# Hybrid decoder trunk on one core: scores and values of the local attentions joined in pairs of head pairs, in other PSUM banks, with two buffers of flipped probabilities

## The chip, the core and the metric

The kernel runs on one core of one Trainium2 chip. The metric is the device time of one execution in microseconds; the median of three runs of the kernel before is 823.28 us (823.21 to 823.98).

## What is computed

Two layers of a decoder trunk on 256 tokens of width 1024. Each layer has three sub-layers, each with an RMSNorm before and after it and a residual: a hybrid mixer, a cross-attention into 256 memory tokens, and a gated feed-forward network with a short convolution. The change is in the mixer. Its input projection feeds a stick-breaking attention (4 heads of 64), a convolution module, and a dilated local attention (8 heads of 64, three windows merged), and their outputs are joined in front of one output projection:

```python
def hybrid_mixer(h, positions, w_in, ...):
    u = h @ w_in
    ...
    a_out = stick_breaking_attention(sb[:, :, 0], sb[:, :, 1], sb[:, :, 2])
    b_out = conformer_conv(...)
    q = rope(dl[:, :, 0], positions)
    k = rope(dl[:, :, 1], positions)
    c_out = dilated_mixture(q, k, dl[:, :, 2])
    return jnp.concatenate([a_out, b_out, c_out], axis=-1) @ w_out
```

With 256 tokens the three windows of the local attention come down to one softmax: a score counts as often as there are windows that hold it (0 to 3), so the exponentials are multiplied by a table of counts before they are summed.

## The kernel before

The program is written out by hand for each engine, with semaphores; no planner sets an order. All weights come as 256 groups of 512 KB through a ring of four buffers. ScalarE rounds a group to a high part (`whi`, `split_group`, L544), VectorE subtracts that for the low part (`wlo`, L955), and TensorE multiplies in three passes (high times high, high times low, low times high). A group is 24 matmuls of 256 columns where the result is wanted by feature (`transposed_product`, L1602 to L1604), 12 of 512 columns where it is wanted by token (`product`, L1585 to L1587), and 24 of 256 columns for the stick values (L1862 to L1864). TensorE frees a buffer with `w_used`; ScalarE splits run three groups ahead (`AHEAD`).

Between the weight products TensorE does the attention, in float32. The 8 local heads are taken as 4 pairs c = 0 to 3, the two heads r = 0, 1 of a pair on the upper and the lower 64 rows (or columns) of the array. For each pair:

- `dl_scores(c)` (L1717): scores of both heads, r = 0 in one bank of `psAB` and r = 1 in the other. For c > 0 each head waits for `nb_ready`, the maxima of the pair before, because the banks are the same.
- `scores_max(c)` on VectorE (L1188): adds the mask while copying the scores to SBUF (one of two buffers, by c % 2), takes the row maxima, and publishes the negated maxima (`nb_ready`).
- `exp_pair(c)` on ScalarE (L659), then `probabilities(c)` on VectorE (L1202): times the counts, sums, reciprocals (L1212, `den_ready`), then `scale_pair(c)` on ScalarE (L668, rows L673): probabilities, `p_ready`.
- `dl_flip(c)` on TensorE (L1725, rows L1532): six transposes into the two banks of `psCD`; `p_columns(c)` on ScalarE (L676) copies them to the one buffer `pT`, for which it waits until the values of the pair before are done (`o_done`).
- `dl_values(c)` on TensorE (L1730, rows L1734 and L1735): both heads into one half of the bank `accs[1][1]` (`attended`); `mixed_hi` (L683) and `mixed_lo` (L1214) take the result off in two parts for the output projection, and the next `dl_values` waits for them (`mix_lo`).

The order on TensorE: scores 0, product, scores 1, product, flip 0, scores 2, product, values 0, flip 1, scores 3, product, values 1, flip 2, first half of the stick values' weight product, values 2, stick scores 0 (`sb_scores`, L1742), second half, flip 3, product (memory keys), values 3, product, and then the cumulative sums of the stick-breaking (`sb_between`), its second pair of scores, and its values (`sb_values(0)` into `accs[0][0]`, `sb_values(1)` into `psAB[1]`). The stick scores need `sbT`, which ScalarE copies (`transposed_in`, L652) after `p_columns(2)`. VectorE has in the same stage 31 taps of the convolution (`conv_taps`, L1235, two instructions a tap) and the low parts.

Of the kernel before, what the change touches and what calls it, by code (L numbers as in the profile page):

```python
# [20 lines left out]
ACT = mybir.ActivationFunctionType  # L21
# [3 lines left out]
P = 128  # L25
DEPTH = 2
D = 1024
SEQ = 256
TOK = SEQ // P
KC = D // P  # L30
# [115 lines left out]
def hybrid_trunk(nc, x, mem, pos, consts, gains, params, pw, stream, out):  # L146
    with ExitStack() as ctx:
# [70 lines left out]
        pT = part(2 * AW).rearrange("p (h n) -> p h n", h=2)  # L218
# [48 lines left out]
        attended = accs[1][1][:, 0:SEQ]  # L267
# [91 lines left out]
        o_done = signal("o_done", DL_HEADS // 2)  # L359
# [7 lines left out]
        sbo_done = signal("sbo_done", 2)  # L367
        mix_hi = signal("mix_hi", KC)
        mix_lo = signal("mix_lo", KC)
# [158 lines left out]
        def _(act):  # L528
# [54 lines left out]
            for l in range(DEPTH):  # L583
# [180 lines left out]
                mixed_hi(4, o_done, 1, attended)  # L764
# [4 lines left out]
                mixed_hi(5, o_done, 2, attended)  # L769
# [3 lines left out]
                mixed_hi(6, o_done, 3, attended)  # L773
# [5 lines left out]
                mixed_hi(7, o_done, 4, attended)  # L779
# [6 lines left out]
                mixed_hi(0, sbo_done, 1, accs[0][0][:, 0:SEQ])  # L786
# [3 lines left out]
                mixed_hi(1, sbo_done, 2, psAB[1][:, 0:SEQ])  # L790
# [150 lines left out]
        def _(dve):  # L941
# [113 lines left out]
            for l in range(DEPTH):  # L1055
# [132 lines left out]
                def scores_max(c):  # L1188
                    w = 4 * (c % 2)
                    for r in range(2):  # L1190
# [4 lines left out]
                        for q, (a, b) in enumerate(((0, P), (P, AW))):  # L1195
                            e = dve.tensor_tensor_reduce(sms[c % 2][r][:, a:b], psAB[r][:, a:b], negm[:, a:b], 1.0,
# [17 lines left out]
                def mixed_lo(n, chunk, src, bias=None):  # L1214
                    dve.wait_ge(mix_hi.sem, mix_hi.at(l, n))
                    cols = slice(chunk * SEQ, (chunk + 1) * SEQ)
# [127 lines left out]
                mixed_lo(3, 6, attended)  # L1344
# [6 lines left out]
                mixed_lo(4, 7, attended)  # L1351
# [12 lines left out]
                mixed_lo(5, 0, accs[0][0][:, 0:SEQ])  # L1364
# [11 lines left out]
                mixed_lo(6, 1, psAB[1][:, 0:SEQ])  # L1376
# [793 lines left out]
```

## Time and profile before

| | |
|---|---|
| median of three runs | 823.28 us |
| the profiled execution | 823.6 us |
| its span | 821.5 us |
| TensorE busy | 812.9 us, 99% |
| VectorE busy | 642.5 us, 78% |
| ScalarE busy | 519.5 us, 63% |
| granted clock of TensorE | 0.999 |
| DMA | 145.69 MB, mean 177 GB/s |

The profile is of one execution. TensorE's rows show when a matmul starts and a modelled duration that overlaps the next; so the time of a group is read from its first start to the first start of what follows. A float32 matmul has two records, so that a pair of scores (four matmuls) has eight. A wait in the middle of a row's group does not show as idle time where the modelled durations cover it. The local attention of layer 0 lies between 73 and 105 us, that of layer 1 between 473 and 506 us.

### The profile page before, as it was taken

The numbers are of one execution on the slowest core, as the hardware profiler recorded it, in microseconds if no ns is written. First come the engines' busy times: TensorE is split into PE (matmuls) and PEld (weight loads), VectorE is DVE, ScalarE is ACT, GpSimd is POOL, SyncE is SP. The second block draws the span as 40 slices with busy tenths as digits, with TensorE's granted clock in tenths as the row PEclk, the third lists the DMA queues.
The fourth block names the chain that finished last, engine by engine and source line by source line (L and its number), as shares of the span: only waits on it lengthen the run. The fifth ranks groups of instructions, "written<-read, shape, count | busy, mean of one in ns | idle before, by whom it ended". The sixth has DMA issues, their size and how long they took to land.

```text
span 821.5 us, 12037 instructions
## 1 busy us (share of the span) xinstructions
PE 812.9 (99%) x4604; PEld 700.1 (85%) x4604; DVE 642.5 (78%) x1129; ACT 519.5 (63%) x809; POOL 29.2 (4%) x54
## 2 busy tenths in 40 slices
PE   8999999999999999999999999999999999999997
PEld 5998888889888888888899889888988888888885
DVE  5899986776676999998386999848677499999753
ACT  5656876566556777765365588656666477776541
POOL 2100000010010000000010000001000000000000
PEclk9999999999999999999999999999999999999999
DMA  8756344472464565556666453446535545655661
GB/s 299 282 177 182 103 128 165 144 259 99 154 233 136 172 203 193 173 197 210 200 197 239 147 154 113 141 157 204 206 121 179 189 128 180 190 174 199 223 189 51
DMA packets 40444, 145.69 MB, mean 177 GB/s; under 512 B 4594, under 2 KB 4738, under 8 KB 40388
## 3 DMA queue, kind: packets, MB, share of 16 engines
q1 hardware_dynamic: 38448, 138.38, 51.0%
q0 software_dynamic: 1936, 6.55, 2.3%
q8 instruction: 36, 0.59, 0.3%
q14 instruction: 20, 0.16, 0.1%
q10 hardware_dynamic: 4, 0.00, 0.0%
HBM read 143.87 MB, written 1.05 MB: 176 GB/s over the span
## 4 chain that ended last, share of the span: by engine, by line
PE 96%; DMA 1%; issue 1%; DVE 1%; ACT 0%; SPq 0%; DVEq 0%; POOLq 0%; POOL 0%
PE acc L1620 8%; PE acc L1587 5%; PE acc L1585 5%; PE acc L1586 5%; PE psCD L1620 4%; PE acc L1629 4%; PE acc L1602 4%; PE acc L1674 4%; PE psAB L1620 4%; PE acc L1676 4%; PE acc L1675 4%; PE acc L1603 3%; PE acc L1604 3%; PE psAB L1587 3%; PE psAB L1585 3%; PE psAB L1586 3%
## 5 line engine op out<-in xcount | busy, mean ns | idle before, releaser
L955 DVE TENSOR_TENSOR wlo<-raw,whi 128x1024 fp32r<-128x1024 f32 x240 | 287.7, 1220 | 70.6 <-ACT whi L544 68.9
L544 ACT ACTIVATE whi<-raw 128x1024 fp32r<-128x1024 f32 x240 | 249.7, 1057 | 120.0 <-PE acc L1587 45.8
L1620 PE MATMUL acc<-xT,whi 128*128 128x512 f32 x288 | 89.2, 391 | 0.0
L1620 PEld LDWEIGHTS acc<-xT,whi 128*128 128x128 f32 x288 | 54.1, 188 | 12.0
L1473 DVE SCALAR_TENSOR_TENSOR KT<-V,par,KT 128x255 f32<-128x255 f32 (+1 forms) x144 | 59.9, 478 | 1.8 <-ACT KT L888 1.2
L1629 PE MATMUL acc<-xT,wlo 128*128 128x256 f32 x288 | 58.1, 284 | 0.0
L1602 PE MATMUL acc<-xT,whi 128*128 128x256 f32 x176 | 51.0, 290 | 0.0
L1235 DVE SCALAR_TENSOR_TENSOR arena<-arena,par 128x256 f32<-128x256 f32 x120 | 50.2, 478 | 0.8 <-ACT arena L740 0.8
L1620 PE MATMUL psCD<-xT,whi 128*128 128x512 f32 x160 | 50.2, 395 | 0.0
L1603 PE MATMUL acc<-xT,whi 128*128 128x256 f32 x176 | 49.8, 283 | 0.0
L1604 PE MATMUL acc<-xT,wlo 128*128 128x256 f32 x176 | 49.8, 283 | 0.0
L471 POOL TENSOR_TENSOR stat<-stat 128x1 f32<-128x1 f32 x30 | 18.8, 626 | 777.3 <-DVE stat L1095 403.3
L1629 PEld LDWEIGHTS acc<-xT,wlo 128*128 128x128 f32 x288 | 44.8, 191 | 0.0
L1620 PE MATMUL psAB<-xT,whi 128*128 128x512 f32 x128 | 39.9, 393 | 0.0
L888 ACT ACTIVATE KT<-V,par 128x256 f32<-128x256 f32 x72 | 37.3, 595 | 0.0
L1602 PEld LDWEIGHTS acc<-xT,whi 128*128 128x128 f32 x176 | 33.7, 191 | 2.9 <-issue 2.6
L594 ACT ACTIVATE junk<-acc 128x512 bf16<-128x512 f32 x20 | 11.8, 591 | 36.9 <-PE acc L1695 22.6
L1587 PE MATMUL psAB<-whi,gT 128*128 128x512 f32 x88 | 34.3, 390 | 0.0
L1585 PE MATMUL psAB<-whi,gT 128*128 128x512 f32 x88 | 34.3, 390 | 0.0
L1586 PE MATMUL psAB<-wlo,gT 128*128 128x512 f32 x88 | 34.3, 389 | 0.0
L1603 PEld LDWEIGHTS acc<-xT,whi 128*128 128x128 f32 x176 | 33.7, 192 | 0.1
L1604 PEld LDWEIGHTS acc<-xT,wlo 128*128 128x128 f32 x176 | 33.7, 191 | 0.0
(312 smaller groups left out, 2049.0 us busy)
## 6 DMA issues: line engine op xcount, KB each, us to landing
raw<-stream_dram SPq DMA_DIRECT2D x256, 512.0 KB, 4.0
gpost<-gain_dram POOLq DMA_DIRECT2D x6, 512.0 KB, 5.1
gpre<-gain_dram POOLq DMA_DIRECT2D x5, 512.0 KB, 5.8
memn<-mem_dram SPq DMA_DIRECT2D x2, 512.0 KB, 10.8
out_dram<-h SPq DMA_DIRECT2D x4, 256.0 KB, 2.1
cst<-const_dram SPq DMA_DIRECT2D x1, 896.0 KB, 6.5
h<-x_dram SPq DMA_DIRECT2D x2, 256.0 KB, 2.8
h<-x_dram SPq DMA_DIRECT2D x1, 512.0 KB, 8.7
```

Of the source, the lines that this page charges most:

```text
L544: act.activation(home(g)[0], raw[:, s * GW:(s + 1) * GW], ACT.Copy).then_inc(w_hi.sem, 1)
L955: dve.tensor_tensor(lo, raw[:, cols], hi.bitcast(F32), ALU.subtract).then_inc(w_lo.sem, 1)
L1235: e = dve.scalar_tensor_tensor(acc, src, w, acc, ALU.mult, ALU.add)
L1473: e = dve.scalar_tensor_tensor(y[:, c, shift:SEQ], u[:, 0:SEQ - shift], par[:, PC_FW + 3 * fc + 1 - k:PC_FW + 3 * fc + 2 - k], y[:, c, shi ...
L1585: pe.matmul(outs[t], a_hi, whi[:, cols], start=k == 0, stop=False)
L1586: pe.matmul(outs[t], a_hi, wlo[:, cols], start=False, stop=False)
L1587: e = pe.matmul(outs[t], a_lo, whi[:, cols], start=False, stop=k == k_of - 1)
L1602: pe.matmul(dst, whi[:, cols], hi[:, toks], start=k == 0 and c % 2 == 0, stop=False)
L1603: pe.matmul(dst, whi[:, cols], lo[:, toks], start=False, stop=False)
L1604: e = pe.matmul(dst, wlo[:, cols], hi[:, toks], start=False, stop=k == KC - 1 and c % 2 == 1)
L1620: e = pe.matmul(up_halves(j, c), whi[:, cols], both, start=k0 + u == 0, stop=closes and u == UNITS - 1)
L1629: e = pe.matmul(up_halves(j, c)[:, 0:SEQ], wlo[:, cols], hi, start=False, stop=False)
```

## The change

It joins the scores of pairs 0 and 1 into one group on TensorE and those of pairs 2 and 3 into another, each pair of heads with banks of its own (`dl_banks`): `psAB`, `psCD`, `psAB` and both banks of `accs[1]`. Scores 1 and 3 no longer wait for maxima; scores 2 wait for those of pair 0, flip 0 for those of pair 1 (it writes the banks that hold scores 1), and values 0 for those of pair 3. The values are joined too, pairs 0 and 1 after the fourth product and pairs 2 and 3 after the first product of the memory keys, into the two halves of `attended`, and taken off by copies of 512 columns. `pT` has two buffers. The two values of the stick-breaking are joined behind the last product of the memory values, both in `psAB[1]`. On VectorE `scores_max(1)` stands right behind `scores_max(0)`, and `scores_max(3)` ahead of `probabilities(2)`. The main parts of the diff:

```diff
         sms = [[sm0[:, 0:AW], sm0[:, AW:2 * AW]], [V[:, NT:NT + AW], V[:, D + NT:D + NT + AW]]]
-        pT = part(2 * AW).rearrange("p (h n) -> p h n", h=2)
+        pT = [part(2 * AW).rearrange("p (h n) -> p h n", h=2) for _ in range(2)]
 
...
+        attended = accs[1][1]
+        sticks = psAB[1]
+
+
+        def dl_banks(c):
+
+            return (psAB, psCD, psAB, accs[1])[c]
 
 
...
                 def p_columns(c):
                     for r in range(2):
                         act.wait_ge(p_tr.sem, p_tr.at(l, 2 * c + r + 1))
-                        if c and not r:
-                            act.wait_ge(o_done.sem, o_done.at(l, c))
-                        act.activation(pT[:, r, :], psCD[r][:, 0:AW], ACT.Copy).then_inc(pT_in.sem, 1)
-
-                def mixed_hi(chunk, ready, n, src, bias=None):
+                        if c >= 2 and not r:
+                            act.wait_ge(o_done.sem, o_done.at(l, 1))
+                        act.activation(pT[c % 2][:, r, :], psCD[r][:, 0:AW], ACT.Copy).then_inc(pT_in.sem, 1)
+
+                def mixed_hi(chunk, ready, n, src, bias=None, chunks=1):
                     act.wait_ge(ready.sem, ready.at(l, n))
-                    act.activation(oT_hi[:, chunk * SEQ:(chunk + 1) * SEQ], src,
+                    act.activation(oT_hi[:, chunk * SEQ:(chunk + chunks) * SEQ], src,
                                    ACT.Copy if bias is None else ACT.Identity,
                                    bias=0.0 if bias is None else bias).then_inc(mix_hi.sem, 1)
...
                 scale_pair(1)
                 exp_pair(2)
                 split(G_SBQK + 3 + AHEAD)
-                mixed_hi(4, o_done, 1, attended)
                 p_columns(1)
                 scale_pair(2)
                 exp_pair(3)
                 split(G_SBV + AHEAD)
-                mixed_hi(5, o_done, 2, attended)
+                mixed_hi(4, o_done, 1, attended, chunks=2)
                 p_columns(2)
                 transposed_in(sbT.rearrange("p c n -> p (c n)"), [a[:, :] for a in accs[0]], G_SBQK + PER_TILE, sbT_in)
                 scale_pair(3)
-                mixed_hi(6, o_done, 3, attended)
...
-                            e = dve.tensor_tensor_reduce(sms[c % 2][r][:, a:b], psAB[r][:, a:b], negm[:, a:b], 1.0,
+                            e = dve.tensor_tensor_reduce(sms[c % 2][r][:, a:b], dl_banks(c)[r][:, a:b], negm[:, a:b], 1.0,
...
                 split(G_DLV + 3 + AHEAD)
                 dve.wait_ge(cst_in.sem, 16)
                 scores_max(0)
+                scores_max(1)
                 split(G_SBQK + AHEAD)
                 probabilities(0)
-                scores_max(1)
                 split(G_SBQK + 1 + AHEAD)
                 probabilities(1)
                 scores_max(2)
                 split(G_SBQK + 2 + AHEAD)
                 conv_taps(15, 16)
-                mixed_lo(1, 4, attended)
+                scores_max(3)
                 probabilities(2)
-                scores_max(3)
                 split(G_SBQK + 3 + AHEAD)
                 conv_taps(16, 17)
-                mixed_lo(2, 5, attended)
+                mixed_lo(1, 4, attended, chunks=2)
                 probabilities(3)
                 conv_taps(17, 19)
                 split(G_SBV + AHEAD)
...
                     for r in range(2):
-                        if c:
-                            pe.wait_ge(nb_ready.sem, nb_ready.at(l, 2 * (c - 1) + r + 1))
+                        if c == 2:
+                            pe.wait_ge(nb_ready.sem, nb_ready.at(l, r + 1))
+                        bank = dl_banks(c)[r]
                         q, k = (a[r * HD:(r + 1) * HD, c, :] for a in (dqT, dkT))
-                        pe.matmul(psAB[r][:, 0:P], q[:, 0:P], k[:, 0:P], start=True, stop=True)
-                        pe.matmul(psAB[r][:, P:AW], q[:, P:SEQ], k, start=True, stop=True).then_inc(s_done.sem, 1)
+                        pe.matmul(bank[:, 0:P], q[:, 0:P], k[:, 0:P], start=True, stop=True)
+                        pe.matmul(bank[:, P:AW], q[:, P:SEQ], k, start=True, stop=True).then_inc(s_done.sem, 1)
 
                 def dl_flip(c):
+                    if c:
+                        pe.wait_ge(pT_in.sem, pT_in.at(l, 2 * c))
+                    else:
+                        pe.wait_ge(nb_ready.sem, nb_ready.at(l, 4))
...
-                        pe.matmul(o[:, 0:SEQ], dlv[:, v0:v0 + HD], pT[:, r, 0:SEQ], start=True, stop=False)
-                        e = pe.matmul(o[:, P:SEQ], dlv[:, NT + v0:NT + v0 + HD], pT[:, r, SEQ:AW],
-                                      start=False, stop=True)
+                def dl_values(pair):
+                    for c in (2 * pair, 2 * pair + 1):
+                        pe.wait_ge(pT_in.sem, pT_in.at(l, 2 * c + 2))
+                        at = c % 2 * SEQ
+                        for r in range(2):
+                            o, v0 = attended[r * HD:(r + 1) * HD, at:at + SEQ], (2 * c + r) * HD
+                            pe.matmul(o[:, 0:SEQ], dlv[:, v0:v0 + HD], pT[c % 2][:, r, 0:SEQ], start=True, stop=False)
...
                 dl_scores(0)
+                dl_scores(1)
                 transposed_product(G_SBQK, 1, X, acc[0])
-                dl_scores(1)
                 transposed_product(G_SBQK + 1, 1, X, acc[0], k0=2)
                 dl_flip(0)
+                pe.wait_ge(dlv_in.sem, dlv_in.at(l, TOK))
                 dl_scores(2)
-                pe.wait_ge(dlv_in.sem, dlv_in.at(l, TOK))
+                dl_scores(3)
                 transposed_product(G_SBQK + 2, 1, X, acc[0], k0=4)
+                dl_flip(1)
+                transposed_product(G_SBQK + 3, 1, X, acc[0], k0=6)
+                pe.wait_ge(nb_ready.sem, nb_ready.at(l, DL_HEADS))
                 dl_values(0)
-                dl_flip(1)
-                dl_scores(3)
-                transposed_product(G_SBQK + 3, 1, X, acc[0], k0=6)
-                pe.wait_ge(mix_lo.sem, mix_lo.at(l, 1))
-                dl_values(1)
                 dl_flip(2)
 
...
                 stick_values(0)
-                pe.wait_ge(mix_lo.sem, mix_lo.at(l, 2))
-                dl_values(2)
-                pe.wait_ge(nb_ready.sem, nb_ready.at(l, DL_HEADS))
                 pe.wait_ge(sbT_in.sem, sbT_in.at(l, 2))
                 sb_scores(0)
                 stick_values(1)
                 dl_flip(3)
                 transposed_product(G_WK1, 1, M, acc[0])
-                pe.wait_ge(mix_lo.sem, mix_lo.at(l, 3))
-                dl_values(3)
+                pe.wait_ge(mix_lo.sem, mix_lo.at(l, 1))
...
                 pe.wait_ge(sbv_in.sem, sbv_in.at(l, 1))
-                pe.wait_ge(mix_lo.sem, mix_lo.at(l, 4))
+                pe.wait_ge(mix_lo.sem, mix_lo.at(l, 2))
                 product(G_WV0, 2, M, acc[1])
-                pe.wait_ge(KT_in.sem, KT_in.at(l, 4))
-                sb_values(0, accs[0][0])
                 sb_between(1)
...
-                sb_values(1, psAB[1])
```

On TensorE, at the start of the local attention (`psAB<-arena` and `psCD<-arena` are scores, `acc<-xT,whi` a weight product), before:

```order
L1587 MATMUL acc<-whi,xT 128x512
L1722 MATMUL psAB<-arena 128x128
L1723 MATMUL psAB<-arena 128x256
L1722 MATMUL psAB<-arena 128x128
L1723 MATMUL psAB<-arena 128x256
L1602 MATMUL acc<-xT,whi 128x256
```

and with the change:

```order
L1587 MATMUL acc<-whi,xT 128x512
L1723 MATMUL psAB<-arena 128x128
L1724 MATMUL psAB<-arena 128x256
L1723 MATMUL psAB<-arena 128x128
L1724 MATMUL psAB<-arena 128x256
L1723 MATMUL psCD<-arena 128x128
L1724 MATMUL psCD<-arena 128x256
L1723 MATMUL psCD<-arena 128x128
L1724 MATMUL psCD<-arena 128x256
L1602 MATMUL acc<-xT,whi 128x256
```

The eight matmuls of scores 0 and 1 stand together, the second four in `psCD`; the product that stood between them follows.

On VectorE, the end of `scores_max(0)` and what follows up to the first reciprocal of pair 0 (rows `stat<-stat 128x2` end a head's maxima or its sums), before:

```order
L1194 MEMSET stat 128x2
L1196 ISA arena,stat<-psAB,cst 128x128
L1196 ISA stat 128x1
L1196 ISA arena,stat<-psAB,cst 128x256
L1196 ISA stat 128x1
L1199 TENSOR_SCALAR stat<-stat 128x2
L955 TENSOR_TENSOR wlo<-raw,whi 128x1024
L1209 ISA arena,stat<-arena,cst 128x128
L1209 ISA stat 128x1
L1209 ISA arena,stat<-arena,cst 128x256
L1209 ISA stat 128x1
L1212 RECIPROCAL stat<-stat 128x2
```

and with the change, the same stretch, from the second head of `scores_max(1)` on:

```order
L1197 MEMSET stat 128x2
L1199 ISA V,stat<-psCD,cst 128x128
L1199 ISA stat 128x1
L1199 ISA V,stat<-psCD,cst 128x256
L1199 ISA stat 128x1
L1202 TENSOR_SCALAR stat<-stat 128x2
L958 TENSOR_TENSOR wlo<-raw,whi 128x1024
L1212 ISA arena,stat<-arena,cst 128x128
L1212 ISA stat 128x1
L1212 ISA arena,stat<-arena,cst 128x256
L1212 ISA stat 128x1
L1215 RECIPROCAL stat<-stat 128x2
```

Both heads of `scores_max(1)` (the first stands just above these rows) now come ahead of the weight split and of the probabilities of pair 0.

## Rows read from the trace of the kernel before

**Rows 1.** The page: busy time, the clock over 40 slices, the chain that ended last.
```profile
PE 812.9 (99%) x4604; PEld 700.1 (85%) x4604; DVE 642.5 (78%) x1129; ACT 519.5 (63%) x809; POOL 29.2 (4%) x54
...
PEclk9999999999999999999999999999999999999999
...
PE 96%; DMA 1%; issue 1%; DVE 1%; ACT 0%; SPq 0%; DVEq 0%; POOLq 0%; POOL 0%
```
**Rows 2.** Timeline of TensorE, layer 0. Columns: start, duration (us), engine, line, operands, count.
```profile
73.10 0.50 PE L1722 MATMUL psAB<-arena 64*128 64x128 f32 x4
...
73.97 0.39 PE L1602 MATMUL acc<-xT,whi 128*128 128x256 f32 x1
...
77.03 0.59 PE L1722 MATMUL psAB<-arena 64*128 64x128 f32 x4
...
80.96 0.82 PE L1532 MATMUL psCD<-cst,arena 128*128 128x128 f32 x6
81.71 0.50 PE L1722 MATMUL psAB<-arena 64*128 64x128 f32 x4
...
82.57 0.39 PE L1602 MATMUL acc<-xT,whi 128*128 128x256 f32 x1
...
91.95 0.88 PE L1532 MATMUL psCD<-cst,arena 128*128 128x128 f32 x6
92.58 0.36 PE L1862 MATMUL acc<-whi,xT 128*128 128x256 f32 x1
...
96.44 0.71 PE L1742 MATMUL psAB<-arena 64*128 64x256 f32 x4
...
97.30 0.39 PE L1862 MATMUL acc<-whi,xT 128*128 128x256 f32 x1
...
103.88 0.66 PE L1734 MATMUL acc<-arena 128*64 128x256 f32 x4
...
104.69 0.39 PE L1602 MATMUL acc<-mT_hi,whi 128*128 128x256 f32 x1
```
**Rows 3.** Timeline of VectorE, layer 0, from the first scores_max on.
```profile
75.22 0.06 DVE L1194 MEMSET stat<- 128x2 f32 x1
...
76.98 1.22 DVE L955 TENSOR_TENSOR wlo<-raw,whi 128x1024 fp32r<-128x1024 f32 x1
78.12 0.29 DVE L1209 CUSTOM_DVE_ANT_0 arena<-arena,cst 128x128 f32<-128x128 f32 x1
...
78.80 0.17 DVE L1212 RECIPROCAL stat<-stat 128x2 f32<-128x2 f32 x1
...
79.54 0.17 DVE L1212 RECIPROCAL stat<-stat 128x2 f32<-128x2 f32 x1
...
87.11 0.87 DVE L1235 SCALAR_TENSOR_TENSOR arena<-arena,par 128x256 f32<-128x256 f32 x2
```
**Rows 4.** Timeline of ScalarE, layer 0, scaling of pair 0 to the stick inputs.
```profile
79.00 1.55 ACT L673 ACTIVATE arena<-arena,stat 128x128 f32<-128x128 f32 x4 [0.94 <-DVE stat L1212]
...
84.47 1.48 ACT L673 ACTIVATE V<-V,stat 128x128 f32<-128x128 f32 x4
...
93.05 1.05 ACT L544 ACTIVATE whi<-raw 128x1024 fp32r<-128x1024 f32 x1
...
94.27 0.86 ACT L681 ACTIVATE arena<-psCD 128x384 f32<-128x384 f32 x2
95.00 1.09 ACT L652 ACTIVATE arena<-acc 128x512 f32<-128x512 f32 x2
```
**Rows 5.** Timelines of TensorE and VectorE, layer 1, same place.
```profile
477.76 0.48 PE L1722 MATMUL psAB<-arena 64*128 64x128 f32 x2
...
478.67 0.49 PE L1722 MATMUL psAB<-arena 64*128 64x128 f32 x2
...
483.23 0.39 PE L1722 MATMUL psAB<-arena 64*128 64x128 f32 x2
...
480.33 0.17 DVE L1212 RECIPROCAL stat<-stat 128x2 f32<-128x2 f32 x1
```

More of the change, by code:

```diff
@@ L358, in hybrid_trunk @@
         pT_in = signal("pT_in", DL_HEADS)
-        o_done = signal("o_done", DL_HEADS // 2)
+        o_done = signal("o_done", DL_HEADS // 4)
         z_done = signal("z_done", 2)
@@ L366, in hybrid_trunk @@
         a_ready = signal("a_ready", 2)
-        sbo_done = signal("sbo_done", 2)
-        mix_hi = signal("mix_hi", KC)
-        mix_lo = signal("mix_lo", KC)
+        sbo_done = signal("sbo_done", 1)
+        mix_hi = signal("mix_hi", 5)
+        mix_lo = signal("mix_lo", 5)
         rows_in = signal("rows_in", 3 * TOK)
@@ L778, in _ @@
                 split(G_WK1 + AHEAD)
-                mixed_hi(7, o_done, 4, attended)
+                mixed_hi(6, o_done, 2, attended, chunks=2)
                 split(G_WK1 + 2 + AHEAD)
@@ L789, in _ @@
                 split(G_WV0 + 3 + AHEAD)
-                mixed_hi(1, sbo_done, 2, psAB[1][:, 0:SEQ])
+                mixed_hi(0, sbo_done, 1, sticks, chunks=2)
                 for c in range(2):
@@ L1350, in _ @@
                 split(G_WK1 + AHEAD)
-                mixed_lo(4, 7, attended)
+                mixed_lo(2, 6, attended, chunks=2)
                 split(G_WK1 + 1 + AHEAD)
@@ L1728, in dl_flip @@
                         flip(psCD[r], sms[c % 2][r], 3).then_inc(p_tr.sem, 1)
-                def dl_values(c):
-                    pe.wait_ge(pT_in.sem, pT_in.at(l, 2 * c + 2))
-                    for r in range(2):
-                        o, v0 = accs[1][1][r * HD:(r + 1) * HD, :], (2 * c + r) * HD
-                        pe.matmul(o[:, 0:SEQ], dlv[:, v0:v0 + HD], pT[:, r, 0:SEQ], start=True, stop=False)
-                        e = pe.matmul(o[:, P:SEQ], dlv[:, NT + v0:NT + v0 + HD], pT[:, r, SEQ:AW],
-                                      start=False, stop=True)
+                def dl_values(pair):
[5 more added lines that the diff above has]
+                            pe.matmul(o[:, 0:SEQ], dlv[:, v0:v0 + HD], pT[c % 2][:, r, 0:SEQ], start=True, stop=False)
+                            e = pe.matmul(o[:, P:SEQ], dlv[:, NT + v0:NT + v0 + HD], pT[c % 2][:, r, SEQ:AW],
+                                          start=False, stop=True)
                     e.then_inc(o_done.sem, 1)
@@ L1754, in sb_between, with sb_values @@
                     e.then_inc(b_done.sem, 1)
-                def sb_values(c, bank):
-                    pe.wait_ge(a_ready.sem, a_ready.at(l, c + 1))
-                    for r in range(2):
-                        o, v0 = bank[r * HD:(r + 1) * HD, :], (2 * c + r) * HD
-                        a = sb_w[c][:, r * AW:(r + 1) * AW]
-                        pe.matmul(o[:, 0:SEQ], sbv[:, v0:v0 + HD], a[:, 0:SEQ], start=True, stop=False)
-                        e = pe.matmul(o[:, P:SEQ], sbv[:, SB_W + v0:SB_W + v0 + HD], a[:, SEQ:AW],
-                                      start=False, stop=True)
+                def sb_values():
+                    pe.wait_ge(a_ready.sem, a_ready.at(l, 2))
+                    for c in range(2):
+                        for r in range(2):
+                            o, v0 = sticks[r * HD:(r + 1) * HD, c * SEQ:(c + 1) * SEQ], (2 * c + r) * HD
+                            a = sb_w[c][:, r * AW:(r + 1) * AW]
+                            pe.matmul(o[:, 0:SEQ], sbv[:, v0:v0 + HD], a[:, 0:SEQ], start=True, stop=False)
+                            e = pe.matmul(o[:, P:SEQ], sbv[:, SB_W + v0:SB_W + v0 + HD], a[:, SEQ:AW],
+                                          start=False, stop=True)
                     e.then_inc(sbo_done.sem, 1)
@@ L1898, in _ @@
                 product(G_WV0 + 2, 2, M, acc[1], k0=4)
-                sb_values(1, psAB[1])
+                sb_values()
                 pe.wait_ge(ln_n.sem, ln_n.at(l, TOK))
@@ L1905, in _ @@
                     e.then_inc(ln_tb.sem, 1)
[L1907 removed]
+                pe.wait_ge(KT_in.sem, KT_in.at(l, 4))
                 product(G_OUT, 1, O, acc[0], order=MIX_ORDER)
```

18 lines of the change are left out of this document (7 added, 11 removed).

## The prediction

> **What bounds the kernel now.** I read the page first, then the order in time of TensorE, VectorE and ScalarE in the stage of the local attention. TensorE is busy for 812.9 of 821.5 us and makes up 96% of the chain that ended last [rows 1]. So only what lengthens or shortens TensorE's own stream counts. The time lies there in small groups of float32 matmuls (scores S, flips F of the probabilities, values V; S0 is the first pair of heads) between weight products of 24 matmuls.
>
> The reader is to see three things in the rows of layer 0 [rows 2]. A product of 24 takes 3.06 us up to the next small group (73.97 to 77.03). S takes 0.86 (73.10 to 73.97, and again 81.71 to 82.57), V 0.81 (103.88 to 104.69). And no small group waits visibly. That is because VectorE and ScalarE, which make the probabilities, are just in time: the scaling of pair 0 starts at 79.00 and ends at 80.55 [rows 4], and F0 starts at 80.96 [rows 2], a margin of 0.4 us. The first half of pair 1's scores, in layer 1, is where TensorE does wait: its two heads start 0.91 apart (477.76 and 478.67 [rows 5]), where in layer 0 the first four records, those of both heads, fit into 0.59 (the row at 77.03 [rows 2]). That wait is for the maxima of pair 0, since pair 1 goes to the same banks.
>
> **Part 1: S1 behind S0, S3 behind S2, in banks of their own.** The wait in layer 1 goes: it is worth 0.9 us. A joined S needs no change to or from the weight product. Its cost in that place is on no row: at most the 0.86 of S, at least the streaming alone. A head streams two records of 128 columns and two of 256, six units of 128, both heads side by side; F has six transposes of 128 columns too and takes 0.63 up to a product (91.95 to 92.58). I take 0.75, midway, since nothing speaks for either end, and the same for a joined V. Little rests on it: most joined groups come ahead of a wait that takes the difference up, and two a layer (V3 and the joined stick values) are left on the path.
> The Trainium skill, TensorEngine Tiling (Array Packing), Key Properties, says that a change of tiling mode drains TensorE; by it a joined group would cost its streaming alone, and with 0.63 for the four groups on the path the sum below would be 828.4 instead of 828.9. No row here shows a joined pair.
> Without waits, TensorE's small groups shrink by about 0.1 for each of two S, two V and the stick values, and by 0.1 to 0.2 for each of the changes to and from a weight product that go with S1, V1 and V2: about 1.0 us a layer, an estimate, 2.0 in all, 2.9 with the wait of layer 1.
>
> **Part 2: the maxima of pair 1 move ahead of the probabilities of pair 0 on VectorE.** This decides. One scores_max takes 1.76 us (75.22 to 76.98 [rows 3]). It now stands before the weight split and the denominators of pair 0, so the reciprocal that ends at 78.97 (78.80 + 0.17) ends at 80.73. ScalarE's scaling, which already waited 0.94 for it [rows 4], starts at 80.76, and its halves (1.55 / 2, the second one released 0.74 later as the reciprocals are, 78.80 to 79.54) end at 81.54 and 82.31. TensorE reaches F0 at about 80.6, because S1 is joined. Its two flips start at 81.6 and 82.36, and half of F (0.75 / 2, 80.96 to 81.71) later S2 starts at **82.73, 1.0 later than before** (81.71). In layer 1 the wait of S1 is gone, but the same reciprocal (480.33 + 0.17 [rows 5]) moves to 482.26, the flips to 483.1 and 483.86 and S2 to 484.23 against 483.23: again 1.0 later. So the wait that layer 1 loses is given back whole; TensorE only arrives earlier at a result that is late.
>
> **Part 3: from S2 to the stick-breaking values.** In times of layer 0:
> S2 and S3 end at 82.73 + 0.86 + 0.75 = 84.34 (before 82.57). The product up to F1 ends at 87.4. ScalarE runs back to back from the scaling of pair 0 to that of pair 1 (79.00 to 84.47 [rows 4]), so this one shifts by 1.76 as well, to 86.23, and its second half is ready at 87.7: F1 loses 0.1 and the next product starts at 88.07 (half of F before a product is 0.31, 91.95 to 92.58 [rows 2]).
> That product ends at 91.13. V0 now waits for the maxima of pair 3, because these scores lie in the bank that the values are written to. VectorE reaches them after two taps: 87.11 + 0.79 + 1.76 = 89.66, and they are published 1.86 later: V0 starts at 91.5, a wait of 0.4. V0 and V1 take 0.81 + 0.75, to 93.1. The probabilities of pair 2 stand behind those maxima, from 91.42; the reciprocal follows 0.85 later (78.12 to 78.97 [rows 3]), the halves of the scaling end at 93.09 and 93.83, and the weight product of the stick values starts at 93.88 + 0.31 = **94.19, 1.6 later than before** (92.58).
>
> **Part 4: the stick scores.** Before, they started at 96.44, right as their input had been copied (95.00 + 1.09 = 96.09 [rows 4]). Now TensorE would reach them at 94.19 + 3.06 = 97.25. ScalarE has first to do, from 92.31 on: scaling of pair 2 (1.46, its row less 0.1 of overlap with the next), exponentials of pair 3 (four instructions of the same sizes, 1.40), a weight split (1.05 less the same overlap), the joined copy of values (0.48, as one of the two copies of 512 columns at 95.00), the flipped probabilities (0.73, 94.27 to 95.00), then the copy itself (1.09): 98.4. That is another wait of 1.2 us, and the stick scores start **2.0 later than before**. In return V2 is gone from ahead of them; that is already in the sum, as they wait for ScalarE either way.
>
> **Part 5: the rest of the layer.** The second joined V adds 0.75 after the first product of the memory keys (2.8 late), the stick values of pair 0 leave their old place (-0.81) and come back joined behind the last product (+0.75), and the transposes for the normalisation may wait 0.1 for the last convolution taps, which are late too: +2.8 us at the output projection. Fewer and wider copies on ScalarE and VectorE are worth nothing on TensorE: they lie beside weight products, except the joined one of part 4, whose cost is in it. The second buffer of flipped probabilities takes away a wait of ScalarE for the values that was not on the path; without it the joined V would not be possible. POOL and the DMA queues have no row that moves, and the transfers of weights are released by VectorE's splits, which stay several products ahead.
>
> **The sum.** 2 x 2.8 = +5.6 us. The profiled execution took 823.6 us (a span of 821.5), 0.3 above the median of 823.28; the sum stands against either alike: 823.28 + 5.6 = **828.9 us**, 0.7% slower. A measurement of this kernel can tell about 0.2%, 1.6 us, from no change.
>
> **Rivals.**
> A, faster: everything is ready in time and only TensorE's saving counts, 823.28 - 2.9 = 820.4. For it: the page, on which TensorE is all. It decides if the reciprocals of pair 0 come less than 0.4 us late. Against it: VectorE has 1.76 us put in front, and ScalarE already waited there [rows 4]. Chance 0.10.
> B, smaller loss: ScalarE catches up before the stick scores (the margin in part 4 is a sum of six terms). Then these start at 97.25, 0.8 late, and the layer ends 1.6 late: 826.4. Chance 0.15.
> C, no change within 1.6 us: besides that only half of the 1.76 us shows, since the split behind it would have waited for ScalarE anyhow; some 0.5 a layer, 824.3. Chance 0.06.
> D, larger loss: lateness of VectorE reaches the stick-breaking part, where softplus, cumulative sums and a second round of scores hang on one another; each layer 1 us more: 831. Chance 0.10.
> E, the clock: the granted clock is 9 tenths or more in all slices [rows 1], so no row prices the lower of its levels. If the waits of part 2 and 4 brought it from 2.4 to 1.2 GHz for the next product, each would cost 3 us more; four of them make 841. The Trainium skill, TensorE: Matmul & The Clock Gate, says that an idle TensorE gets the lower level. No stretch here shows that. Chance 0.02.
> My forecast has 0.57.
>
> **How the numbers follow.** Faster by over 0.2%: A, 0.10. Within 0.2%: C, 0.06. Slower: the forecast, B, D and E, 0.84. The range goes from 0.8 below B to D: 825.6 to 831.2. Outside lie A, C and E, 0.18. It takes in the bounds of the joined groups on the path (0.63 to 0.86, four of them, 0.9 us).
>
> **What would show it.** In the profile after: in each layer F0 split in two with a gap of 0.7 between its heads and a wait of 1 to 2.5 us before it, put down to ScalarE's scaling; ScalarE's idle time before the scaling of pair 0 up from 0.94 to 2.7; a wait of 0.4 before V0 for VectorE; a wait of about 1.2 before the stick scores for ScalarE's copy; S1 in layer 1 without its gap. TensorE's busy time falls a little and its idle time grows by some 5 us. If F0 starts within 0.3 us of its product's end, part 2 is wrong, and with it the sign.

## The result, and the profile after

The changed kernel takes 828.1 us (median of six runs, 828.0 to 828.44), the kernel before in the same comparison 823.17. The ratio is 1.0062 with a 95% interval of 1.0052 to 1.0072: slower by 4.9 us. The forecast was 828.9, in a range of 825.6 to 831.2.

The page of the changed kernel, where [rows 1] stood for the one before (busy time, clock, chain):

```profile
span 826.0 us, 12025 instructions
...
PE 810.1 (98%) x4604; PEld 699.5 (85%) x4604; DVE 642.0 (78%) x1123; ACT 518.3 (63%) x803; POOL 29.3 (4%) x54
...
PEclk9999999999999999999999999999999999999999
...
PE 85%; DVE 9%; ACT 2%; issue 2%; DMA 1%; SPq 0%; POOL 0%; DVEq 0%; POOLq 0%; ACTq 0%
```

TensorE is busy for 2.8 us less than before and the span is 4.5 us longer, so it stands idle for 7.3 us more. In the chain that ended last TensorE has fallen from 96 to 85%, and VectorE has come in with 9%: ahead of the stage in layer 0 the chain now runs through VectorE's convolution taps and weight splits, from 61 us on. The clock, in tenths, is as it was.

The waits of TensorE by line and by who released it (us in total, times, longest), of the changed kernel, those in the local attention:

```profile
PE psCD L1532 <- ACT arena L679: 3.0, 2, 1.9
PE psAB L1749 <- ACT arena L658: 2.3, 2, 1.1
...
PE acc L1741 <- DVE stat L1202: 0.8, 2, 0.4
```

Each has one case in each layer: flips of pair 0 behind ScalarE's scaling, the stick scores behind ScalarE's copy of their input, values 0 behind VectorE's maxima of pair 3. The list of the kernel before has none of the three. This is TensorE's order in time in layer 0 (start, duration, engine, line, operands; in brackets the idle time before it and its releaser), for [rows 2]:

```profile
72.21 0.50 PE L1723 MATMUL psAB<-arena 64*128 64x128 f32 x4
...
72.97 0.49 PE L1723 MATMUL psCD<-arena 64*128 64x128 f32 x4
...
80.87 1.20 PE L1532 MATMUL psCD<-cst,arena 128*128 128x128 f32 x6 [1.03 <-ACT arena L679]
82.01 0.50 PE L1723 MATMUL psAB<-arena 64*128 64x128 f32 x4
...
90.78 0.66 PE L1741 MATMUL acc<-arena 128*64 128x256 f32 x4 [0.42 <-DVE stat L1202]
...
91.48 0.65 PE L1741 MATMUL acc<-arena 128*64 128x256 f32 x4
...
92.44 1.20 PE L1532 MATMUL psCD<-cst,arena 128*128 128x128 f32 x6
93.40 0.36 PE L1869 MATMUL acc<-whi,xT 128*128 128x256 f32 x1
...
97.64 0.71 PE L1749 MATMUL psAB<-arena 64*128 64x256 f32 x4 [1.13 <-ACT arena L658]
...
133.42 0.48 PE L1585 MATMUL acc<-whi,oT_hi 128*128 128x512 f32 x1
```

The stage starts 0.9 us earlier here than in the execution shown of before, so times are to be read from its first scores (72.21; before 73.10). Then the flips of pair 0 and pair 2 are stretched to 1.20 us (0.82 and 0.88 before), because the second head's probabilities come later than the first's; the joined scores take 0.76 for the first pair, the joined values 0.70 (90.78 to 91.48).

ScalarE in the same stretch, for [rows 4]:

```profile
79.93 1.54 ACT L679 ACTIVATE arena<-arena,stat 128x128 f32<-128x128 f32 x4 [2.77 <-DVE stat L1215]
81.38 1.04 ACT L550 ACTIVATE whi<-raw 128x1024 fp32r<-128x1024 f32 x1
...
91.50 1.54 ACT L679 ACTIVATE arena<-arena,stat 128x128 f32<-128x128 f32 x4 [1.53 <-DVE stat L1215]
...
96.50 1.08 ACT L658 ACTIVATE arena<-acc 128x512 f32<-128x512 f32 x2
```

It waits 2.77 us for the first reciprocal of pair 0 (0.94 before) and copies the stick inputs from 96.50 to 97.58. VectorE, for [rows 3]:

```profile
77.92 1.22 DVE L958 TENSOR_TENSOR wlo<-raw,whi 128x1024 fp32r<-128x1024 f32 x1
...
79.73 0.17 DVE L1215 RECIPROCAL stat<-stat 128x2 f32<-128x2 f32 x1
...
82.45 1.23 DVE L958 TENSOR_TENSOR wlo<-raw,whi 128x1024 fp32r<-128x1024 f32 x1 [1.82 <-ACT whi L550]
...
88.86 0.06 DVE L1197 MEMSET stat<- 128x2 f32 x1
```

Its split of the weights at 77.92 comes behind both pairs' maxima, and the next split, at 82.45, waits 1.82 us for ScalarE's half, which stands behind the late scaling (81.38 above). So VectorE loses time to ScalarE, which lost it to VectorE. Without this second wait VectorE would be level with its old order here, since the maxima of pair 1 are already done; with it, it stays 1.8 us late, and begins the maxima of pair 3 at 88.86.

To compare kernels I use one length: from the first scores of the local attention to the first matmul of the output projection (in the rows above 133.42 - 72.21 = 61.21 us), "the stage". The table is taken from times with more digits, so that its last digit can differ by one. All else hardly moves: in the eleven profiles (one of each kernel) the time between the two stages is 342.0 to 342.4 us, and from the end of the second to TensorE's last matmul 282.3 to 282.5. Where the first stage starts varies from one execution to the next, from 70.9 to 73.1 us, with the same instructions of TensorE ahead of it; that is why spans compare less well than stages. The kernels with an e are the experiments of the next section.

| kernel | stage, layer 0 | stage, layer 1 | median | ratio to before, 95% |
|---|---|---|---|---|
| before | 58.57 | 59.47 | 822.4 to 823.2 | |
| the change | 61.20 | 62.11 | 828.1 | 1.0062 (1.0052 to 1.0072) |
| e1_dve_order | 59.41 | 60.34 | 824.2 | 1.0022 (1.0013 to 1.0031) |
| e2_sbt_early | 60.90 | 61.85 | 827.83 | 1.0069 (1.0055 to 1.0083) |
| e4_s1_bank_only | 58.48 | 59.31 | 822.15 | 0.9997 (0.9988 to 1.0006) |
| e5_dve_order_only | 62.25 | 61.19 | 827.53 | 1.0058 (1.0046 to 1.0071) |
| e6_s1_bank_and_tap | 58.48 | 58.50 | 821.33 | 0.9988 (0.9979 to 0.9997) |
| e7_joined_late_s1 | 58.66 | 59.52 | 822.88 | 1.0004 (0.9995 to 1.0013) |
| e8_dve_order_and_tap | 58.67 | 59.54 | 822.88 | 1.0006 (0.9997 to 1.0015) |
| e9_sbt_behind_scale2 | 57.71 | 58.55 | 821.08 | 0.9982 (0.9973 to 0.9991) |
| e10_all_mended | 57.69 | 58.32 | 820.47 | 0.9975 (0.9966 to 0.9985) |

The change costs 2.63 us in one stage and 2.64 in the other, 5.3 together. The median of before was 823.17 in the comparison with the change and 822.4 in all others, so kernels of different comparisons are best set side by side by their ratios.

### The profile page after: what moved, and what is told of

It is laid out like the page before. It is cut to its first block, busy times and chain, and to the rows that moved or that the text cites. A ratio compares the mean times of both kernels' runs of the same rounds, so it can differ in the third digit from the quotient of the medians.

```text
span 826.0 us, 12025 instructions
## 1 busy us (share of the span) xinstructions
PE 810.1 (98%) x4604; PEld 699.5 (85%) x4604; DVE 642.0 (78%) x1123; ACT 518.3 (63%) x803; POOL 29.3 (4%) x54
## 4 chain that ended last, share of the span: by engine, by line
PE 85%; DVE 9%; ACT 2%; issue 2%; DMA 1%; SPq 0%; POOL 0%; DVEq 0%; POOLq 0%; ACTq 0%
PE acc L1620 8%; PE psCD L1620 4%; PE acc L1586 4%; PE acc L1585 4%; PE acc L1587 4%; PE acc L1629 4%; PE acc L1674 4%; PE psAB L1620 4%; PE acc L1676 4%; PE acc L1675 4%; PE psAB L1587 3%; PE psAB L1586 3%; PE psAB L1585 3%; DVE wlo L958 3%; PE acc L1602 3%; PE acc L1604 3%
## 5 line engine op out<-in xcount | busy, mean ns | idle before, releaser
L1238 DVE SCALAR_TENSOR_TENSOR arena<-arena,par 128x256 f32<-128x256 f32 x120 | 50.3, 480 | 0.8 <-ACT arena L746 0.8
```

The lines of the kernel that those rows point to most:

```text
L1238: e = dve.scalar_tensor_tensor(acc, src, w, acc, ALU.mult, ALU.add)
```

## The experiments

My theory was that the loss comes from VectorE's order alone, that joining on TensorE is a small gain, and that a wait shown by TensorE need not be worth what it shows. The rivals were a loss in the joined groups, waits that simply add up, and an amount of work on VectorE that no order changes.

**VectorE's old order in the changed kernel (e1).**

```diff
                 scores_max(0)
-                scores_max(1)
                 split(G_SBQK + AHEAD)
                 probabilities(0)
+                scores_max(1)
                 split(G_SBQK + 1 + AHEAD)
```

> The changed kernel with one thing put back: on VectorE scores_max(1) stands behind probabilities(0) again. Theory 1 (the loss comes from VectorE's order: pair 0's reciprocals 1.76 us late, and then VectorE itself waits 1.9 us for a weight split that ScalarE does behind the late scaling): F0 waits for the maxima of pair 1 instead of the probabilities and starts about 0.5 us earlier, the waits at F1, V0 and F2 go, only the one before the stick scores stays at about 1.2; 1.8 us a layer come back, 824.5 us. Rival (TensorE's waits are set by the work that VectorE has in sum before the maxima of pair 3, which is the same in either order): the wait at V0 takes up what F0 gains, nothing comes back, 828 us. Rival 2 (the loss is in the joined groups or their banks on TensorE): nothing comes back either, and the waits stay small.

It came to 824.2 us (by the ratios 3.3 us less than the change), and the stages are 1.79 and 1.77 us shorter than with the change. TensorE's order in time in layer 0:

```profile
79.31 0.87 PE L1532 MATMUL psCD<-cst,arena 128*128 128x128 f32 x6 [0.82 <-DVE stat L1202]
...
88.32 0.66 PE L1741 MATMUL acc<-arena 128*64 128x256 f32 x4
...
94.45 0.71 PE L1749 MATMUL psAB<-arena 64*128 64x256 f32 x4 [0.89 <-ACT arena L658]
```

VectorE there, the first maxima of pair 3:

```profile
85.67 0.06 DVE L1197 MEMSET stat<- 128x2 f32 x1
```

The flips are whole again (0.87), now behind the maxima of pair 1, the wait at the values of pair 0 is gone, and the one before the stick scores stays at 0.89. Theory 1 had said 1.8 a layer and 824.5 us. The maxima of pair 3 do not come at the same time in either order: they begin 14.81 us into the stage (85.67 - 70.86, its first scores) against 16.65 in the changed kernel (88.86 - 72.21), since the 1.82 us in which VectorE stood waiting for ScalarE go too. So neither rival explains these 1.8 us. But the order of these two lines is not the whole loss, as my theory had it: e1 is still 0.84 and 0.87 us a stage behind the kernel before. What it keeps of the change is the flips' wait for the maxima of pair 1, and the maxima of pair 3 ahead of the probabilities of pair 2: the first reciprocal of pair 2 starts 17.25 us into the stage, before at 16.49, and ScalarE's scaling and its copy of the stick inputs follow. No run puts that second order back by itself.

**VectorE's new order in the kernel before (e5).** The kernel before with the same two lines exchanged the other way, and the scores of pair 1 in the banks of `accs[1]` so that VectorE can have them early (their own effect is the next run's).

> The kernel before with the banks of the last run and VectorE's new order alone: scores_max(1) ahead of the split and of probabilities(0), nothing joined on TensorE. Theory 1 (VectorE's order is the loss): F0 starts some 2 us late, since VectorE also stands idle until the scores of pair 1 are there; 2.6 us more in layer 0 and 1.8 in layer 1, 827.6 us. Rival (the loss is in the joining on TensorE): 823 us.

827.53 us, with stages 3.77 and 1.88 us longer than in e4, which differs from it in VectorE's order alone. No group is joined here. In layer 1 the order costs what it cost in the changed kernel (1.8 between that and e1); layer 0 is a case of its own, below. VectorE's idle times in layer 0:

```profile
77.21 0.06 DVE L1197 MEMSET stat<- 128x2 f32 x1 [0.95 <-PE acc L1727]
...
83.50 1.22 DVE L958 TENSOR_TENSOR wlo<-raw,whi 128x1024 fp32r<-128x1024 f32 x1 [1.82 <-ACT whi L547]
```

The 0.95 us are VectorE waiting for the scores of pair 1, which no longer stand right behind those of pair 0. The 1.82 us behind ScalarE's split appear again. In layer 0 TensorE loses more than its waits. Its rows in time there:

```profile
81.83 0.55 PE L1535 MATMUL psCD<-cst,arena 128*128 128x128 f32 x3 [1.61 <-ACT arena L676]
82.57 0.55 PE L1535 MATMUL psCD<-cst,arena 128*128 128x128 f32 x3 [0.20 <-ACT arena L676]
...
85.27 0.41 PE L1605 MATMUL acc<-xT,whi 128*128 128x256 f32 x1
85.49 0.41 PE L1606 MATMUL acc<-xT,whi 128*128 128x256 f32 x1
...
86.75 0.28 PE L1606 MATMUL acc<-xT,whi 128*128 128x256 f32 x1
86.86 0.28 PE L1607 MATMUL acc<-xT,wlo 128*128 128x256 f32 x1
```

Behind the flips the product's matmuls start 0.21 us apart until 86.6, and 0.12 (as everywhere else) after it. The busy times by stretch (engine sums and counts, then the granted clock as a share of 2.4 GHz, then DMA) say why:

```profile
78.00:82.00 4.00, 2.39 (x21) 2.19 (x20) 3.52 (x18) 1.03 (x3) 0.00 (x0) 1.00 0.15 39
83.00:86.60 3.60, 3.60 (x20) 2.90 (x19) 2.98 (x15) 3.60 (x9) 0.00 (x0) 0.54 0.24 55
87.00:90.00 3.00, 3.00 (x28) 2.51 (x26) 2.86 (x10) 3.00 (x8) 0.00 (x0) 1.00 0.19 75
```

The granted clock is 0.54 in the middle one, so for nearly all of it at the lower level, 1.2 GHz. In slices of 0.2 us it is 1.00 up to 83.2, 0.50 in each slice from 83.4 to 86.6, and 1.00 again from 86.8. The scores of pair 2 take 1.42 us for 0.86, the product behind them 4.03 for 3.05: 1.5 us. This is the prediction's rival E, in a kernel of mine. In layer 1 the same waits of 1.61 and 0.20 stand in front of the same instructions, and the matmuls behind are 0.12 apart. The medians of e5 and e4 are 5.4 us apart and their stages 5.65, where with 1.9 in each layer it would be 3.8. The five timed executions fall into two groups: 827.53, 827.78 and 828.01 us (the profiled one), with a mean granted clock of 0.997, and 826.18 and 826.55 us, with 0.998. The second group is 4.0 and 4.4 us above the median of e4, so by all appearance the clock fell in three of the five and not in the other two; only one of them has a trace. What VectorE's order costs without the fall is about 1.9 us a layer.

**The scores of pair 1 in banks of their own, alone (e4).** The part of the change that takes away the wait of 0.9 us in layer 1:

```diff
+        def dl_banks(c):
+            return accs[1] if c == 1 else psAB
...
-                        if c:
-                            pe.wait_ge(nb_ready.sem, nb_ready.at(l, 2 * (c - 1) + r + 1))
+                        if c >= 2:
+                            pe.wait_ge(nb_ready.sem, nb_ready.at(l, (4 if c == 3 else 0) + r + 1))
...
+                pe.wait_ge(dlv_in.sem, dlv_in.at(l, TOK))
                 dl_scores(1)
...
+                pe.wait_ge(nb_ready.sem, nb_ready.at(l, 4))
                 dl_values(0)
```

> The kernel before with one part of the change alone: the scores of pair 1 go to the two banks of accs[1], in their old place, so that they need not wait for the maxima of pair 0; values 0 wait for the maxima of pair 1 (long done). Theory 1 (the wait of 0.9 us in layer 1 is worth what it shows): 822.3 us. Theory 2 (ScalarE's train to the stick inputs sets the time there, TensorE only arrives earlier and waits at the flips or at values 2): no change, 823.2 us, with small waits at F0, F1 and V2 in layer 1 that sum to 0.9.

The ratio is 0.9997 (0.9988 to 1.0006), and the stage of layer 1 is 0.16 us shorter. TensorE in layer 1:

```profile
475.34 0.50 PE L1726 MATMUL acc<-arena 64*128 64x128 f32 x4
...
479.18 1.18 PE L1535 MATMUL psCD<-cst,arena 128*128 128x128 f32 x6
480.29 0.50 PE L1726 MATMUL psAB<-arena 64*128 64x128 f32 x4
...
494.51 0.66 PE L1738 MATMUL acc<-arena 128*64 128x256 f32 x4 [0.22 <-ACT arena L684]
494.96 0.42 PE L1739 MATMUL acc<-arena 128*64 128x128 f32 x4
495.48 0.71 PE L1746 MATMUL psAB<-arena 64*128 64x256 f32 x4
```

and before, for the flips of pair 0:

```profile
482.49 0.82 PE L1532 MATMUL psCD<-cst,arena 128*128 128x128 f32 x6
```

The scores of pair 1 are in one piece, 0.50 for the four records that took 0.91 from head to head before [rows 5]. But the flips of pair 0 are stretched to 1.18 (0.82 at this place before), the values of pair 2 wait 0.22 and the stick scores behind them start 0.97 after them where 0.81 is usual. TensorE arrives earlier and waits elsewhere: theory 2. The wait in [rows 5] was worth next to nothing by itself.

**The stick inputs copied earlier (e2).** In the changed kernel, ScalarE's `transposed_in` of the stick inputs moves from behind `p_columns(2)` to right behind `p_columns(1)`, where ScalarE stands idle for 1.53 us.

> The changed kernel with one copy moved on ScalarE: the stick inputs (transposed_in) are copied right after the flipped probabilities of pair 1, where ScalarE stands idle for 1.5 us before the scaling of pair 2. Theory 1 (the waits add up along TensorE, each is worth what it shows): the wait of 1.1 us before the stick scores goes in both layers, 825.8 us. Theory 2 (behind that wait stands the next one, VectorE's convolution taps before the transposes for the normalisation, already 0.2 late): of 1.1 a layer only about 0.4 comes back, 827.3 us, and a wait of some 0.9 us shows before those transposes.

The wait of 1.1 us is gone in both layers, and the stages are only 0.30 and 0.26 shorter; the ratio, 1.0069 (1.0055 to 1.0083), cannot be told from that of the change. (The profiled execution, at 827.34, is the fastest of five. Three of the others have a mean granted clock of 0.996 where it has 1.0, and take 827.83 to 828.63 us; they have no trace.) TensorE's waits:

```profile
PE psAB L1749 <- DVE arena L1263: 0.5, 2, 0.3
...
PE psCD L1897 <- DVE arena L1238: 0.5, 2, 0.2
```

Both are new, and both are VectorE's: the cumulative sums of the stick-breaking (L1263) and the convolution taps before the transposes for the normalisation (L1238). Theory 2 named the second, and at 0.9 us where it is 0.2; the lateness is shared out over both.

**One tap out of VectorE's way (e6).** To go with e4's banks. In layer 1 VectorE reaches its first maxima later than in layer 0, 3.0 us into the stage against 2.1. The ranges of `conv_taps` between the products are each shifted by one tap, so that one is done less before `scores_max(0)` and one more behind the second stick scores:

```diff
-                conv_taps(13, 15)
+                conv_taps(13, 14)
                 split(G_DLV + 3 + AHEAD)
...
-                conv_taps(26, 30)
+                conv_taps(25, 30)
                 sb_keep(1)
```

> The kernel before with the scores of pair 1 in the banks of accs[1] (as in e4_s1_bank_only, which changed nothing) and one tap of the convolution, 0.8 us of VectorE, moved from ahead of scores_max(0) to behind the second stick scores, where VectorE stands idle for 0.8. Theory 1 (in layer 1 VectorE's start of the maxima sets the stage, and the bank alone could not help because of it): the two together save 0.8 us in layer 1 and nothing in layer 0, where TensorE waits nowhere; 0.9990 of before, 821.6 us. Rival (ScalarE's own work, not its start, sets the time to the stick inputs): no change.

821.33 us, ratio 0.9988 (0.9979 to 0.9997). The stage of layer 1 falls by 0.81 against e4, to 58.50, that of layer 0 stays at 58.48: both are now TensorE's own work without a wait. In layer 1 VectorE now begins 2.2 us into the stage. The same tap without the banks was not tried, so that no run shows whether the banks have a part in these 0.81 us or whether the tap gives them alone.

**The changed kernel repaired in steps (e8, e7, e9, e10).** e8 is e1 with that tap:

> The changed kernel with VectorE's old order (as e1_dve_order) and the tap moved as in e6. Theory 1 (what is left of the loss in e1 is VectorE's and ScalarE's lateness at F0 and at the stick scores, 0.9 in each): the tap gives 0.8 back in each layer, 822.6 us, close to before. Rival: F0 waits for the maxima of pair 1 whatever VectorE does before, and the wait moves there; 824 us as e1.

822.88 us; 0.74 and 0.80 us less a stage than e1, as theory 1 had it. The wait at the flips is gone in layer 0 and down to 1.0 in layer 1; the one before the stick scores stands at 0.9. e7 has besides the scores of pair 1 unjoined, in the banks of `accs[1]` like those of pair 3, so that the flips do not write the banks that hold them:

> The changed kernel rebuilt by what was found: VectorE's old order, the scores of pair 1 alone in their old place in the banks of accs[1], so that F0 need not wait for their maxima; pairs 2 and 3 joined, values joined in pairs as in the change, and the tap moved as in e6. Theory 1 (joining saves about 0.15 to 0.3 us a place on TensorE where nothing waits; the waits were all of VectorE's and ScalarE's lateness): some 0.5 us less than before in layer 0, 1.3 in layer 1, 820.5 us. Rival (with the values joined behind the maxima of pair 3 ScalarE's train is late for the stick scores in any order): 822 to 823 us with a wait of 0.5 or more before the stick scores.

Here the rival was right: 822.88, like e8, and still 0.9 us or more before the stick scores. TensorE arrives there earlier than before, since the values of pair 2 no longer stand ahead, and ScalarE's copy comes when it came. So both got the copy moved, and VectorE's waiting with it:

```diff
                 scale_pair(2)
+                transposed_in(sbT..., G_SBQK + PER_TILE, sbT_in)
                 exp_pair(3)
                 split(G_SBV + AHEAD)
                 mixed_hi(4, o_done, 1, attended, chunks=2)
                 p_columns(2)
-                transposed_in(sbT..., G_SBQK + PER_TILE, sbT_in)
...
-                mixed_lo(1, 4, attended, chunks=2)
+                conv_taps(16, 18)
                 probabilities(3)
-                conv_taps(16, 18)
+                mixed_lo(1, 4, attended, chunks=2)
```

> e8_dve_order_and_tap with the stick inputs copied on ScalarE right behind the scaling of pair 2, ahead of the exponentials of pair 3, and on VectorE mixed_lo(1) behind probabilities(3), with two taps ahead, so that VectorE does not stand waiting for ScalarE's later copy of the values. Theory 1 (in e8 the wait of 0.9 us before the stick scores is the only loss left in layer 0, and with VectorE's order mended there is no next wait at the transposes as there was in e2): 0.9 us less a layer, 0.998 of before, 820.9 us. Rival (as in e2, the lateness only moves to VectorE's taps or to the cumulative sums): 822 to 823 us.

> e7_joined_late_s1 with the same two moves. Theory 1: as e9 in layer 0, and in layer 1 no wait at F0, since the scores of pair 1 are in other banks; small waits at V0 and F2 in layer 1 stay; stage of about 57.7 and 58.2 us against 58.57 and 59.47 before; 820.3 us, 0.9975 of before, and less than e6. Rival: the stage stays at 58.5 us, as in e6, because ScalarE and VectorE have no more room than that.

e9 came to 821.08 and e10 to 820.47 us, 0.9975 of before (0.9966 to 0.9985): faster than both kernels of this study. TensorE's waits in e10, all of them:

```profile
PE acc L1557 <- POOL idle L480: 1.3, 1, 1.3
PE psAB L1563 <- DMA arena<-gain_dram: 0.8, 1, 0.8
PE psAB L1935 <- DVE qT_lo L1404: 0.4, 2, 0.2
PE acc L1791 <- ACT xT L572: 0.2, 1, 0.2
PE acc L1791 <- ACT whi L550: 0.2, 1, 0.2
```

None of them lies in the stage (L1935 is the cross-attention, the rest is the start); in e9 the flips of pair 0 in layer 1 still wait 1.0 for the maxima of pair 1. Layer 1's stage is still 0.6 us longer than layer 0's, in pieces too short for this list: the values of pairs 0 and 1 start 0.15 later there and take 0.17 longer, and the flips of pair 2 take 0.96 instead of 0.63. Its 57.69 us in layer 0 against 58.57 are what joining is worth where nothing waits: 0.88 us a layer, with the scores of pairs 2 and 3, the values in pairs and the stick values joined, and the scores of pair 1 not. A move of the same copy that gave 0.3 in e2 gave 0.96 and 0.99 in e9 (57.71 and 58.55 against e8). The two are not the same edit: e9 has the copy one step later on ScalarE, VectorE's order and tap mended, and `mixed_lo` moved as well. That VectorE is no longer late behind it fits the waits, of which the stage of layer 0 has none left; which of the edits does it, no run separates.

## Why the prediction was right

Taken against the first scores of each stage in layer 0, step by step:

- **Part 2** put the scores of pair 2 at 1.0 us late. They start 9.80 us into the stage (82.01 - 72.21) where before it was 8.61: 1.2. The scaling waits 2.77 where 2.7 was forecast, and the two flips are apart as said. In layer 1 it is 1.2 as well, though the wait of the scores of pair 1 is gone there. e1 and e5 show that this order is the cause of the late scaling and of 1.8 us of the loss in each layer.
- **Part 3** had a wait of 0.4 before the values (0.42), a joined V of 0.75 (0.70), and the stick values' product 1.6 late: 21.19 against 19.48, 1.7. One step in it has no reason given: VectorE's two taps ahead of the maxima of pair 3 were put 1.76 late, though by then the maxima of pair 1, moved ahead, are done in either order. The number came out right (the maxima at 16.65 us into the stage, forecast 89.66 - 73.10 = 16.56) because VectorE waits 1.82 us for ScalarE's split, a wait of nearly the same size that this part does not name.
- **Part 4** had a wait of 1.2 before the stick scores and these 2.0 late: 1.13, and 25.43 against 23.34, 2.1.
- **Part 5** ended at 2.8 us a layer; measured 2.63. The wait of 0.1 at the transposes did not come, and the joined V were cheaper by 0.05 each.
- **The sum** was 5.6; the stages give 5.3 and the medians 4.9.
- **Rival A** had 2.9 us to be saved without waits. The saving exists, but it is 2.0 us against the kernel before (58.57 and 59.47 down to 57.69 and 58.32; the medians give 1.95), not where the change put it, and one part of it is mis-stated, as follows.
- **The signs.** The waits named under "What would show it" all came, within 0.1 us of their number or in their range. TensorE's idle time was to grow by some 5 us and grew by 7.3: idle time grows by the loss (4.5 us of the span) and by what the busy time falls (2.8), and the second was left out.

Two statements of the prediction were wrong, and did not show in the sum. Part 1 said of the wait in layer 1 "it is worth 0.9 us"; e4 took it away alone and 0.16 came back. (Part 2 said the gain would be given back whole, but gave the changed order as the reason. It is given back without that order too; in layer 1 VectorE reaches its first maxima late, and e6 gained only with that mended.) And rival B took the wait before the stick scores to be worth 1.2 us in each layer if it went (2.8 late down to 1.6); e2 took it away and 0.3 came back. Behind both waits stood the next one.

The cost of a joined S was on no row, and was put between 0.63 and 0.86. The trace has 0.76 for the first of two and 0.86 for the last, which is followed by the change to a weight product. By the rule of the Trainium skill, TensorEngine Tiling (Array Packing), Key Properties, that a change of tiling mode drains TensorE, this is as it should be; if all of the difference is the change, it costs 0.10 us here.

The gap between the two heads' flips is, as part 2 had it, VectorE's 0.74 between the reciprocals (79.73 and 80.47 in the changed kernel), passed on by ScalarE.

Rival E, the clock, had a chance of 0.02. Its "No stretch here shows that" overlooks one in the trace of the kernel before, where TensorE stands idle behind its last matmul (at 815.57):

```profile
819.00:820.00 1.00, 0.00 (x0) 0.00 (x0) 0.02 (x1) 0.00 (x0) 0.00 (x0) 0.53 0.79 293
```

In the profiled execution of the changed kernel the clock did not fall in the stages, though the longest wait of all stands there, 1.93 us before the flips of pair 0 in layer 1:

```profile
481.00:485.00 4.00, 2.21 (x19) 2.01 (x17) 3.71 (x20) 1.11 (x4) 0.00 (x0) 1.00 0.25 68
486.00:490.00 4.00, 4.00 (x36) 3.45 (x35) 3.16 (x15) 4.00 (x10) 0.00 (x0) 1.00 0.33 79
```

The granted clock is 1.00 before and behind it. Of its six timed executions three have a mean granted clock of 0.996 or 0.997, where none on record of the kernel before is under 0.998; they took 828.0 us like the others, and without a trace it stays open whether the clock fell in them. In e5 it happened once in two like places, after shorter waits, and cost 1.5 us where the prediction put 3. By the rule of the Trainium skill, TensorE: Matmul & The Clock Gate, Part 1, an idle TensorE gets the lower level. The end of the kernel before agrees with 0.53, and layer 0 of e5 with 0.54; layer 1 of e5 and the changed kernel show that waits of this length do so only sometimes. What decides was not tried. A chance of 0.02 was too small.

## What to carry to other kernels

On an engine that is full to 99%, look at how early the results that it takes are ready, before its work is rearranged: here they were 0.4 us ahead of use, and 1.76 us put in front of one of them cost 1.8 of the 2.6 us a layer, through a second engine that handed the delay back. A wait in the profile is worth what it shows only if nothing behind it is late by the same cause; take it away alone and measure (0.9 us gave 0.16, 1.1 us gave 0.3), then move the next releaser as well. Joining paid in the end (e10 is 0.25% faster than before, its interval clear of no change), once the producers' orders had been moved to fit it and the scores of pair 1 taken out again.

## What was not expected of the hardware

With the same instructions of TensorE ahead of it the first stage starts between 70.9 and 73.1 us in the eleven profiles, while the time between the stages holds within 0.4 us; most of what sets these executions apart outside the stages is made in the first 70 us. The same waits of 1.61 and 0.20 us before the same matmuls were followed by a granted clock of 0.50 from 83.4 to 86.6 us in one layer of e5 and of 1.00 in the other. Scores on half the rows take 0.10 us more with a full product behind them than with another pair behind them, and joined values take 0.70 where a single pair takes 0.81.
